# A streaming encoder step on one core: attention transposes and what follows them one product later, the first normalisation's factors spread tile by tile, the last means inside the last products

## The reference

```
h = rmsnorm(x, g1); z = h @ w_in          # 16 column groups: mLSTM q,k,v,o,gates; conv b,c,x; attention q,k,v; 3 branch gates
ya = sigmoid(mo) * rmsnorm(mlstm(q, k, v, i, f))
yb = sb * dwconv3(sc * sx)
w1, w2 = softmax(q1 k1^T), softmax(q2 k2^T)       # block-causal for the 512, all 1056 keys for the 32
o = (w1 - lam * w2) @ v;  yc = rmsnorm(o, da_g) * (1 - 0.2)
x = x + (sum_b sigmoid(gt_b) * (y_b @ w_branch_b)) @ w_out
h2 = rmsnorm(x, g2); up = dwconv3(h2 @ w_up)
x = x + (silu(up[:, :2816]) * up[:, 2816:]) @ w_down
y = rmsnorm(x, norm_f)
```

## Time and profile before

| | |
|---|---|
| executions | 999.03, 1000.32, 1001.5 us; median 1000.32 us |
| profiled execution | 1000.77 us, its span 999.0 us |
| PE (matmul) busy | 975.5 us, 98% of the span |
| PEld (weight load) busy | 952.6 us, 95% |
| DVE busy | 692.0 us, 69% |
| ACT busy | 473.0 us, 47% |
| POOL busy | 161.2 us, 16% |
| mean granted TensorE clock | 0.996 of full speed |
| chain that ended last | PE 85%, DVE 6%, issue 4%, ACT 4%, POOL 1% |
| moved by DMA | 99.87 MB, mean 100 GB/s |

### The profile page before, as it was taken

One profiled execution on the slowest core, in us unless ns is written; L12 is line 12 of the kernel. 1 busy time (PEld: TensorE's weight loads), 2 busy tenths in 40 slices (PEclk: granted clock), 3 DMA queues, 4 the chain that ended last, 5 costly groups with the idle time before them and its releaser, 6 DMA issues.

```text
span 999.0 us, 20129 instructions
## 1 busy us (share of the span) xinstructions
PE 975.5 (98%) x7763; PEld 952.6 (95%) x7763; DVE 692.0 (69%) x1161; ACT 473.0 (47%) x982; POOL 161.2 (16%) x343
## 2 busy tenths in 40 slices
PE   7999999999999998999999999999999999999996
PEld 6999899999999998999999999999999999999996
DVE  6887666687667898777775547777777777533353
ACT  5675555576555665655553433333333333322241
POOL 2000121110121221121112211111121111111000
PEclk9999999999999999999999999999999999999998
DMA  6522243364231222233244222222222223323342
...
DMA packets 104086, 99.87 MB, mean 100 GB/s; under 512 B 4868, under 2 KB 99481, under 8 KB 103735
## 3 DMA queue, kind: packets, MB, share of 16 engines
...
## 4 chain that ended last, share of the span: by engine, by line
PE 85%; DVE 6%; issue 4%; ACT 4%; POOL 1%; DMA 0%; DVEq 0%; POOLq 0%; ACTq 0%
PE D L1719 46%; PE D L1776 28%; PE D L1736 2%; DVE w_l L1305 2%; ACT w_h L1009 1%; PE X L1988 1%; PE X L2026 1%; PE D L1828 1%; PE D L1748 1%; DVE ups L1675 1%; PE D L1880 1%; PE X L1934 1%; DVE acc L1685 0%; PE X L1935 0%; PE X L1937 0%
## 5 line engine op out<-in xcount | busy, mean ns | idle before, releaser
L1305 DVE TENSOR_TENSOR w_l<-raw,w_h 128x512 fp32r<-128x512 f32 (+1 forms) x286 | 201.0, 720 | 111.2 <-ACT w_h L1009 109.4
L1776 PE MATMUL D<-a_h,w_h 128*128 128x272 f32 x840 | 250.4, 298 | 3.0 <-DVE tmp L1486 1.6
L1776 PE MATMUL D<-a_h,w_l 128*128 128x272 f32 x840 | 243.0, 289 | 0.0
L1776 PE MATMUL D<-a_l,w_h 128*128 128x272 f32 x840 | 241.6, 288 | 0.0
L1009 ACT ACTIVATE w_h<-raw 128x512 fp32r<-128x512 f32 (+1 forms) x286 | 171.5, 618 | 101.0 <-PE D L1719 77.8
L1776 PEld LDWEIGHTS D<-a_h,w_h 128*128 128x128 f32 x840 | 158.1, 188 | 8.4 <-DVE tmp L1486 3.0
L1776 PEld LDWEIGHTS D<-a_l,w_h 128*128 128x128 f32 x840 | 158.4, 189 | 0.0
L1776 PEld LDWEIGHTS D<-a_h,w_l 128*128 128x128 f32 x840 | 158.0, 188 | 0.0
L1719 PE MATMUL D<-h_h,w_h 128*128 128x272 f32 x704 | 145.9, 288 | 0.1
L1719 PE MATMUL D<-h_h,w_l 128*128 128x272 f32 x704 | 145.7, 288 | 0.0
L1719 PE MATMUL D<-h_l,w_h 128*128 128x272 f32 x704 | 145.1, 288 | 0.0
...
## 6 DMA issues: line engine op xcount, KB each, us to landing
...
```

The source lines that it names most:

```text
L1305: v.tensor_tensor(split_view(w_l, g), whole_view(g), split_view(w_h, g).bitcast(F32), ALU.subtract)\
L1776: last = t.matmul(out, wt[:, k, :], x[:, left, k, :], start=w in (1, 2, 5) and k == i == 0, stop=k == KQ - 1 and i == 2, skip_group_check= ...
```

## The change

Four things are changed.

1. In the attention units the steps `t`, `wt`, `o`, `sq`, `rr`, `on`, `y`, `yt` and `yc` come one product later; `s`, `mx`, `ex` and `wd` stay.
2. The factor of a tile of x is spread right behind the transposes of the next tile (`spread_tile`), into one bank for the first three tiles of 128 and another for the fourth and the 32. ACT copies 384 columns once four factors are there, and the last 160 after `rstd`.
3. `mean 0` and `mean 1` are no longer steps of PE's own but are put into the middle of the last two half products, before the twelfth of their 22 steps (`mean_of_halves`). VectorE's part of `mean 1` comes behind the last half product's addition.
4. In the last `scale`, the two engines share the work otherwise: VectorE takes tile 2, the right half of tile 3 and the right half of the 32 rows; ScalarE the left halves of tile 3 and of the 32 rows. SP stores the right half of tile 3, ScalarE the left half and the 32 rows.

```diff
@@ -136,8 +136,8 @@
         at_time(time, *step)
     for u in range(17):
         t0, t1 = (99 + 28 * (x // 4) + (0, 5, 11, 18)[x % 4] if x >= 0 else 91 for x in (u - 1, u))
-        for dt, sub in ((0, "s"), (1, "mx"), (2, "ex"), (3, "wd"), (5.5, "t"), (6.5, "wt"), (8, "o"), (9, "sq"),
-                        (9, "rr"), (11.5, "on"), (t1 - t0 + 8, "y"), (t1 - t0 + 9, "yt"), (t1 - t0 + 9, "yc")):
+        for dt, sub in ((0, "s"), (1, "mx"), (2, "ex"), (3, "wd"), (6.5, "t"), (7.5, "wt"), (9, "o"), (10, "sq"),
+                        (10, "rr"), (12.5, "on"), (t1 - t0 + 9, "y"), (t1 - t0 + 10, "yt"), (t1 - t0 + 10, "yc")):
             if u or dt > 2:
                 at_time(t0 + dt, "at", sub, u)
 
@@ -229,9 +229,9 @@
     unit("mean", 0)
     unit("yTh", KD - 1, 0)
     unit("yTh", KD - 2, 1)
-    unit("mean", 1)
     unit("scale", 0)
     add("dnh", KD - 1, 1)
+    unit("mean", 1)
     unit("yTh", KD - 1, 1)
     unit("mean", 2)
     unit("scale", 1)
@@ -779,11 +779,9 @@
                     .then_inc(raw_in[i % NRAW], 16)
 
             for i, (c, cols) in enumerate(((0, slice(0, DM)), (1, slice(0, DM)), (2, slice(0, DM // 2)),
-                                           (2, slice(DM // 2, DM)))):
+                                           (2, slice(DM // 2, DM)), (3, slice(DM // 2, DM)))):
                 sp.wait_ge(S["y_dve"], i + 1)
                 sp.dma_start(y_p[0, P * c:P * c + P, cols], yst[:, c, cols]).then_inc(S["y_out"], 16)
-            sp.wait_ge(S["y_dve"], 5)
-            sp.dma_start(y_s[0], yst_s[0:TS, :]).then_inc(S["y_out"], 16)
             sp.wait_ge(S["y_out"], 7 * 16)
             sp.wait_ge(S["out_k"], 64)
             sp.wait_ge(S["out_v"], 64)
@@ -1031,13 +1029,17 @@
                 if kind == "rstd" or (kind == "norm" and a[0] == 1):
 
                     if kind == "rstd":
+                        act.wait_ge(S["sq_x"], 5)
+                        act.wait_ge(S["spread_done"], 1)
+                        sc.activation(rstd[0][:, 0:3 * P], X[:, 2, 0:3 * P], ACT.Copy, scale=float(DM))
                         act.wait_ge(S["dense_done"], n + 1)
-                        r, src, done = 0, banks(n), "act_drained"
+                        sc.activation(rstd[0][:, 3 * P:T], X[:, 3, 0:P + TS], ACT.Copy, scale=float(DM))\
+                            .then_inc(S["act_drained"], 1)
                     else:
                         act.wait_ge(S["rstd_mm"], 1)
-                        r, src, done = 1, X[:, 2:4, :], "rstd_ready"
-                    sc.activation(rstd[r][:, 0:TP], src[:, 0, :], ACT.Copy, scale=float(DM))
-                    sc.activation(rstd[r][:, S0:T], src[:, 1, 0:TS], ACT.Copy, scale=float(DM)).then_inc(S[done], 1)
+                        sc.activation(rstd[1][:, 0:TP], X[:, 2, :], ACT.Copy, scale=float(DM))
+                        sc.activation(rstd[1][:, S0:T], X[:, 3, 0:TS], ACT.Copy, scale=float(DM))\
+                            .then_inc(S["rstd_ready"], 1)
                 elif kind == "lam":
                     act.wait_ge(S["lam_dve"], 2)
                     sc.activation(lam_e[:], lam_e[:], ACT.Exp).then_inc(S["lam_act"], 1)
@@ -1105,12 +1107,15 @@
                 elif kind == "scale" and a[0] == 1:
                     act.wait_ge(S["rs_ready"], 3)
                     act.wait_ge(S["y_copied"], KD + 2)
-                    for i in range(2):
-                        cols = slice(DM // 2 * i, DM // 2 * (i + 1))
-                        sc.activation(yst[:, 3, cols], yst[:, 3, cols], ACT.Copy, scale=ssx[:, 3:4])\
-                            .then_inc(S["y_act"], 1)
-                        act.wait_ge(S["y_act"], i + 1)
-                        act.dma_start(y_p[0, 3 * P:4 * P, cols], yst[:, 3, cols]).then_inc(S["y_out"], 16)
+                    cols = slice(0, DM // 2)
+                    sc.activation(yst[:, 3, cols], yst[:, 3, cols], ACT.Copy, scale=ssx[:, 3:4]).then_inc(S["y_act"], 1)
+                    sc.activation(yst_s[0:TS, cols], yst_s[0:TS, cols], ACT.Copy, scale=ssx[0:TS, 4:5])\
+                        .then_inc(S["y_act"], 1)
+                    act.wait_ge(S["y_act"], 1)
+                    act.dma_start(y_p[0, 3 * P:4 * P, cols], yst[:, 3, cols]).then_inc(S["y_out"], 16)
+                    act.wait_ge(S["y_act"], 2)
+                    act.wait_ge(S["y_dve"], 6)
+                    act.dma_start(y_s[0], yst_s[0:TS, :]).then_inc(S["y_out"], 16)
                 elif kind == "p" and a[1] in (1, 6, 7, 4):
                     q, w = a
                     blk, half = {1: (0, 0), 6: (1, 0), 7: (1, 1), 4: (0, 1)}[w]
@@ -1454,11 +1459,13 @@
                     dve.wait_ge(S["rs_ready"], 2 + a[0])
                     dve.wait_ge(S["y_copied"], KD + 2 * a[0])
                     for c, cols in ((0, slice(0, DM)), (1, slice(0, DM))) if a[0] == 0 else \
-                            ((2, slice(0, DM // 2)), (2, slice(DM // 2, DM))):
+                            ((2, slice(0, DM // 2)), (2, slice(DM // 2, DM)), (3, slice(DM // 2, DM))):
                         v.tensor_scalar(yst[:, c, cols], yst[:, c, cols], ssx[:, c:c + 1], None, ALU.mult)\
                             .then_inc(S["y_dve"], 1)
                     if a[0]:
-                        v.tensor_scalar(yst_s[0:TS], yst_s[0:TS], ssx[0:TS, 4:5], None, ALU.mult).then_inc(S["y_dve"], 1)
+                        cols = slice(DM // 2, DM)
+                        v.tensor_scalar(yst_s[0:TS, cols], yst_s[0:TS, cols], ssx[0:TS, 4:5], None, ALU.mult)\
+                            .then_inc(S["y_dve"], 1)
                 elif kind in ("yT", "yTh"):
                     j, x = a[0], 2 * (a[0] % 2)
                     dve.wait_ge(S["y_tr"], y_event[(kind, *a)] + 1)
@@ -1791,6 +1798,19 @@
                     last = t.matmul(out[0:L, c:c + 1], src[:, col:col + L], mean_w[:, 0:1], start=True, stop=True)
                 last.then_inc(S["norm_mm"], 1)
 
+            def mean_of_halves(part):
+
+                pe.wait_ge(S["sq_added"], KD - 1 + KD - 2)
+                pe.wait_ge(S["sq_done"], KD + KD - 2 + 2 + (part + 1 if part else 0) - (part > 0))
+                out = D[:, (1, 3, 1)[part], :]
+                for c in HALF_TILES[min(part, 1)]:
+                    col, L = TILES[c]
+                    for i in ((0, 1, 2), (0, 1), (2,))[part]:
+                        source = (ssum[2][:], tmp_of(("sq", 2, KD - 2)), tmp_of(("sq", 2, KD - 1)))[i]
+                        last = t.matmul(out[0:L, c:c + 1], source[:, col:col + L], mean_w[:, 0:1],
+                                        start=i in (0, 2 * (part // 2)), stop=i == (2, 1, 2)[part])
+                last.then_inc(S["norm_mm"], 1)
+
             def spread_rstd(out, before, tiles):
                 for i, c in enumerate(tiles):
                     L = TILES[c][1]
@@ -1798,6 +1818,13 @@
                     last = t.matmul(out[:, c // 4, P * (c % 4):P * (c % 4) + L], mean_w[0:L, :],
                                     diag[0:L, c, 0:L], start=True, stop=True)
                 return last
+
+            def spread_tile(i):
+
+                c, L = X_ORDER[i], TILES[X_ORDER[i]][1]
+                out = X[:, 2, P * c:P * c + P] if c < 3 else X[:, 3, P * (c - 3):P * (c - 3) + L]
+                pe.wait_ge(S["diag_ready"], i + 1)
+                return t.matmul(out, mean_w[0:L, :], diag[0:L, c, 0:L], start=True, stop=True)
 
             def turn_over(times, out=X[:, 3, :]):
                 for _ in range(times):
@@ -1828,23 +1855,18 @@
                         last = t.transpose(B[:, j // 4, P * (j % 4):P * (j % 4) + L], src[:, P * j:P * j + P],
                                            ident[0:L, 0:L])
                     last.then_inc(S["dense_done"], 1)
+                    i = X_ORDER.index(c)
+                    if i:
+                        last = spread_tile(i - 1)
+                        if i == 4:
+                            last.then_inc(S["spread_done"], 1)
                 elif kind == "rstd":
-                    spread_rstd(B, 0, X_ORDER).then_inc(S["dense_done"], 1)
+                    spread_tile(4).then_inc(S["dense_done"], 1)
                     for m in waits_of[block_of[("if",)]]:
                         wait_drained(pe, m)
                     turn_over(9, banks(block_of[("if",)])[:, 0, :])
-                elif kind == "mean":
-
-                    pe.wait_ge(S["sq_added"], KD - 1 + KD - 2)
-                    pe.wait_ge(S["sq_done"], KD + KD - 2 + 2 + (a[0] + 1 if a[0] else 0) - (a[0] > 0))
-                    out = D[:, (1, 3, 1)[a[0]], :]
-                    for c in HALF_TILES[min(a[0], 1)]:
-                        col, L = TILES[c]
-                        for i in ((0, 1, 2), (0, 1), (2,))[a[0]]:
-                            source = (ssum[2][:], tmp_of(("sq", 2, KD - 2)), tmp_of(("sq", 2, KD - 1)))[i]
-                            last = t.matmul(out[0:L, c:c + 1], source[:, col:col + L], mean_w[:, 0:1],
```

(7 more changed lines are left out.)

2 lines of the change are left out of this document (1 added, 1 removed).

## The result

The changed kernel took **1002.15 us** in the median of 11 executions (1001.66 to 1004.25). Beside it the kernel before took 1000.18 us (998.58 to 1001.87, 11 executions). The medians lie 1.97 us apart. The ratio is 1.0026, with a 95% interval of 1.0017 to 1.0035, which makes 2.6 us. By either figure the kernel is slower by less than the 3 us that were named as the limit of what can be told, but 1 lies outside the interval. The forecast was 998.2 us, with 995.0 to 1000.9 as its range.

What follows compares the result with a forecast made beforehand. TensorE, busy for 98% of the span, was taken as the bound. End of products 0.85, stores 0.5, start 0.2 and attention 0.6 sum to 2.15 us off, from a median of 1000.32 to 998.2 us; range 995.0 to 1000.9.

Steps and rivals of the forecast that it cites:

- Attention, the failed step: Attention units outside the three places where PE waited for the difference of the maps: moving their steps wins 0.
- 345: Attention at 345.23 us, PE's wait of 1.14 us: ScalarE's pair leaves its place ahead of the exponentials, 0.6 us won.
- 384: Attention at 384.46 us, PE's wait of 0.57 us: the product behind still waits for its bank, 0 won.
- 399: Attention at 399.27 us, PE's wait of 0.91 us: VectorE and the bank come 0.55 us later, 0 won in the end.
- Start: Start of the span: `f_x` starts at 13.98 in place of 14.20, 0.2 us won; bounds 0.3 lost to 0.5 won.
- the caught-up half: Start: PE brings the third tile some 0.7 us late, half caught up; VectorE's last copy ends at 13.65, not 13.40.
- End of the products: Last half products with the means inside: 0.85 us won, 1.6 from the clock less 0.75 of uncovered wait.
- The low clock costs 1.6 us: Last half product of the kernel before: 9.81 us for 65 steps, against 8.2 at the high clock.
- Stores: Last scaling and stores at the span's end: 0.5 us won, bounds 0.1 and 0.9.
- the large store: End of the span: last large store issued 0.55 us earlier; its landing ended the span, so the gain was taken near it.
- Slower: Rival, attention: moved pair or `wt` delays weight copies on ScalarE, 0.59 us per unit; 1004.7 us at 10 units; chance 0.06.
- The clock's rival: Last half product: the clock falls all the same, 1.6 us of low clock, 999.8 us; chance 0.15.

Runs made afterwards that it cites:

- e2: The kernel before, with only unit 0's steps behind its scores one product later; 1003.38 us against 1000.55, ratio 1.0027.
- e5: The kernel before, with only unit 0's averages and what follows them (square, reciprocal, norm) one product later; one execution, 1001.5 us.
- e8: The change with the old start, unit 0 of the attention unshifted, and the first means back between the half products; 998.2 us, ratio 0.9979 to the kernel before.
- e13: The kernel before with attention units 7 and 8 alone one product later (output transposes of 6 and 7 too) and e8's end; 997.6 us, ratio 0.9971.

## Why the prediction was wrong

- **Attention, the failed step:** "The other 13 units show no wait on PE at these steps, so moving them wins nothing." That they win nothing was right for most of them; that they cost nothing was assumed with it, and unit 0, the seventeenth, is in no term of the sum. Its move cost 2.85 us (e2). Nothing waited there before because ScalarE's copy stood ahead of the product's copy and was done while PE worked on that product, and because the averages were early enough for `merged`. The move put the copy behind the product's copy (1.6 us of waiting ahead of unit 1's scores) and the averages behind these scores (1.2 us, e5). The questions that were left out: for each moved step, who waits for it next, also in another unit, and what covers it now; and where each step really lands in the list, since unit 0's `t` stayed and its `wt` did not. The wait `at_wt` ahead of the scores of unit 1 stood in the code.
- **345:** 0.6 forecast, 0.84 measured. The pair left ScalarE's queue ahead of the exponentials as forecast, which accounts for 0.59. That the size came near is partly luck: an earlier copy of a product (0.8 us) and a new wait of 0.3 us for the maximum were in no term. **384:** 0 forecast, 0.39 won. **399:** 0 forecast, 0.36 lost; the wait of 1.50 us at 405.02 in place of 0.5 was not foreseen. Together 0.87 against 0.6.
- **Start:** 0.2 to be won, 0.43 lost. The mis-sized term is the caught-up half. The spreads took some 0.5 us each as estimated, but VectorE did not catch up: its copies of the second, third and fourth tile of 128 start 0.75, 0.84 and 0.84 us later than before, counted from PE's first transpose, where 0.25 was forecast for the last. It waited 1.04 us for PE ahead of the copy of the second tile, and the rate of the loads rose 0.54 us later in this execution (6.67 us behind the first transpose, 6.13 before). `f_x` was bound by VectorE, as forecast. The loss lies outside the bound of 0.3.
- **End of the products:** 0.85 forecast, 0.65 by the ruler from 970 on (2.20 to 1.55). The signs were right and the sum closes: the low clock cost 1.53 us by e5, not 1.6; the transposes between the half products, no longer covered, take 0.71 us more (the wait in brackets is 0.61), for 0.75; and each group of means costs 0.08 us more inside a product than between two, because the matmul behind it starts that much later. The clock stayed at 1.00 through the last half product. But the low clock was taken from one execution, and the median of before is a mixture: 58 of its 91 executions that these batches list have a mean clock of 0.996 or less, and all of these take 1000.2 us or more. The step "The low clock costs 1.6 us" should have been weighted by how often it comes.
- **Stores:** 0.5 forecast, about 0.2: from the last large product to the span's end 9.4 in place of 9.6 us. The term rested on the large store, taken to be issued 0.55 us earlier (994.83 less 994.25 is 0.58). But the store of the 32 rows is now the last: it is issued at 996.22 less 1.55, 0.16 us earlier than the last one before, and its 128 KB took 3.7 us to land (L1118), the same as the longest of the two 256 KB stores before. Half the size won nothing.
- **Rivals:** "Slower" had the right sign and the wrong mechanism (ScalarE's queue at many units): it was one unit, whose copy out of two banks came to stand behind a product's copy, and whose averages came late. The clock's rival did not come true in the 13 profiles with either new order of the means. The Trainium skill, page "TensorE: Matmul & The Clock Gate", section "Part 4: PE-mode transpose", says that transposes don't count as activity in the way that matmuls do. The end fits this only in part: 1.8 us of one-column matmuls and transposes in e8's profile brought no fall, 2.8 us in three of four profiles of the old order did. The start speaks against the rule: in e13 the weight loads of x's transposes go from 230 to 142 ns with nothing but transposes ahead of them.
